# The expert loop's buffers move off the gate buffer, the first blocks' last gates are read on chip, and ScalarE's queue carries the last write-out

## The reference, cut to what matters

```python
def peer(h, w_query, sub_keys, expert_u, expert_v):        # 16384 experts of one neuron each
    q = (hf @ w_query).reshape(T, N_PEER_HEADS, 2, PEER_KEY_DIM // 2)
    s = jnp.einsum('thpk,hpnk->thpn', q, sub_keys)
    s1, i1 = lax.top_k(s[:, :, 0], PEER_TOPK)
    s2, i2 = lax.top_k(s[:, :, 1], PEER_TOPK)
    ...
    top_s, pos = lax.top_k(cand, PEER_TOPK)
    g = jax.nn.softmax(top_s.astype(jnp.float32), axis=-1).astype(h.dtype)
    ...
        a = jax.nn.gelu(jnp.einsum('tkd,td->tk', expert_u[ix], hx), approximate=False)
        return jnp.einsum('tk,tkd->td', gx * a, expert_v[ix])
```

## Time and profile before

| what | value |
|---|---|
| median of 3 runs | 1886.51 us (1883.4 to 1887.89) |
| the profiled execution | 1885.99 us, its span 1884.2 us |
| busy: PE, PEld, DVE, ACT, POOL | 92%, 79%, 78%, 36%, 51% |
| mean granted TensorE clock | 0.971 |
| DMA over the span | 520.92 MB, mean 276 GB/s |
| gate phase ends, loop's first scores, first sums | 751.4, 758.6, 791.0 us |
| last matmul of the loop | about 1848 us |

### The profile page before, as it was taken

The page is one execution under the profiler, slowest core; times in us unless marked ns, Lnnn a source line. Parts: engine busy times, 40 slices in busy tenths (PEclk is TensorE's granted clock), DMA queues, the critical chain, the costliest instruction groups (busy, mean ns, idle before and its releaser), DMA issues.

```text
span 1884.2 us, 29934 instructions
## 1 busy us (share of the span) xinstructions
PE 1739.1 (92%) x9942; PEld 1486.7 (79%) x9942; DVE 1474.6 (78%) x2936; ACT 683.9 (36%) x1145; POOL 961.2 (51%) x838
## 2 busy tenths in 40 slices
PE   5999988699799998499999999999999999999994
PEld 2767656377788886399999999999898998999993
DVE  0732057247968665799999999999999998999997
ACT  1222146110166768133333333333333333333331
POOL 1111000000067687288777777777566665666661
PEclk8999999899999999699999999999999999999997
DMA  9455110500006555999999999999999999999993
GB/s 356 154 198 218 46 57 1 212 23 13 23 1 133 116 111 118 297 392 406 406 407 395 407 407 407 407 407 407 388 403 399 403 402 390 389 405 407 406 406 136
DMA packets 253576, 520.92 MB, mean 276 GB/s; under 512 B 113987, under 2 KB 131011, under 8 KB 252229
## 3 DMA queue, kind: packets, MB, share of 16 engines
q1 hardware_dynamic: 178048, 249.00, 37.3%
q0 software_dynamic: 73728, 268.47, 36.0%
q10 hardware_dynamic: 1734, 2.60, 0.4%
HBM read 488.55 MB, written 31.46 MB: 276 GB/s over the span
## 4 chain that ended last, share of the span: by engine, by line
PE 52%; DVE 20%; issue 12%; DMA 8%; ACT 3%; SPq 2%; DVEq 1%; POOL 1%; POOLq 0%; PEldq 0%; ACTq 0%
PE ps L1758 9%; PE ps L1757 9%; PE ps L1756 9%; DVE arena L1331 9%; PE ps L1632 6%; DMA U_in<-in_expert_uT 4%; DVE V_lo L1273 4%; PE ps L1683 4%; PE ps L1613 3%; DMA arena_w<-in_w_mod 2%; PE ps L1461 2%; PE ps L1462 2%; PE ps L1465 2%; PE ps L1509 1%; DMA arena_w<-in_w_in 1%
## 5 line engine op out<-in xcount | busy, mean ns | idle before, releaser
L1756 PE MATMUL ps<-hT_hi,U_hi 128*128 128x384 f32 x1024 | 344.3, 336 | 7.8 <-DVE arena L1124 7.8
L1758 PE MATMUL ps<-hT_hi,U_lo 128*128 128x384 f32 x1024 | 344.3, 336 | 0.0
L1757 PE MATMUL ps<-hT_lo,U_hi 128*128 128x384 f32 x1024 | 343.7, 336 | 0.0
L1756 PE MATMUL ps<-V_hi,C_hi 128*128 128x512 f32 x768 | 301.7, 393 | 29.3 <-DVE C_lo L1308 29.3
L1758 PE MATMUL ps<-V_hi,C_lo 128*128 128x512 f32 x768 | 303.6, 395 | 0.0
L1757 PE MATMUL ps<-V_lo,C_hi 128*128 128x512 f32 x768 | 303.1, 395 | 0.0
L506 POOL DMA_INDIRECT arena<-in_expert_u,idxn x128 | 176.4, 1378 | 74.3 <-issue 38.2
L506 POOL DMA_INDIRECT arena<-in_expert_v,idxn x128 | 160.6, 1254 | 104.0 <-DVE arena L1331 55.4
L1756 PEld LDWEIGHTS ps<-hT_hi,U_hi 128*128 128x128 f32 x1024 | 192.8, 188 | 12.9 <-issue 8.0
L856 ACT ACTIVATE act_t<-ps 128x384 f32<-128x384 f32 x128 | 63.0, 492 | 368.9 <-PE ps L1758 368.8
L1757 PEld LDWEIGHTS ps<-hT_lo,U_hi 128*128 128x128 f32 x1024 | 192.8, 188 | 4.9
(11 more groups left out here) (240 smaller groups left out, 3237.6 us busy)
## 6 DMA issues: line engine op xcount, KB each, us to landing
U_in<-in_expert_uT SPq DMA_DIRECT2D x128, 512.0 KB, 9.5
V_in<-in_expert_v SPq DMA_DIRECT2D x128, 512.0 KB, 6.6
arena_w<-in_w_mod SPq DMA_DIRECT2D x12, 2048.0 KB, 12.0
gate_in<-gates_scratch SPq DMA_DIRECT2D x128, 192.0 KB, 7.8
gates_scratch<-arena_w SPq DMA_DIRECT2D x5, 4096.0 KB, 21.4
arena_w<-in_w_in SPq DMA_DIRECT2D x4, 2048.0 KB, 8.8
arena_w<-in_w_query SPq DMA_DIRECT2D x1, 7168.0 KB, 21.0
arena_w<-in_w_out SPq DMA_DIRECT2D x2, 2048.0 KB, 10.4
```

The costliest lines, as they stand in the source:

```text
L1756: nc.tensor.matmul(out, hi, rhi, start=start, stop=False)
L1757: nc.tensor.matmul(out, hi, rlo, start=False, stop=False)
L1758: return nc.tensor.matmul(out, lo, rhi, start=False, stop=stop)
```

## The change

- `V_in`, `V_hi`, `gate_in` and `act_t` go to the place of `h2T` and two of the `lhs1` buffers, `V_lo` to the place of the ranking's scratch, `C_hi` and `C_lo` to the place of `lhs1` and `rhs1`. In `gbuf`'s place lie now `rows_late`, `H2s`, `fing` and `XF`. `gbuf`'s first four columns stay free (`first_gates`).
- The last half write-out is one DMA, issued by ScalarE after the last eviction.
- For n = 0 to 3 the gates come in two DMAs: 320 tokens from HBM (`spilled_gates`) and the last 64 straight from `gbuf` (`fresh_gates`). SyncE's first turns are written out by hand; the loop begins at 3. `H2s` is loaded before it.
- SyncE's `break` still stands behind the wait for the last eviction.
- GpSimd's seventh row waits for the whole write-out, as before.
- VectorE ranks all four groups among the last block's gate rows, then come hT_lo and both U_lo with a quad between them, then `select` with two quads. ScalarE makes both `U_hi` at quad 20 and the last exponential at quad 28.
- VectorE waits for the last product and gates ahead of `split_v(0, 0)`.

```diff
...
@@ -181,6 +180,23 @@
...
         w_hi = [w_hi_first] + [w_hi_next] * (IN_CH - 1)
+        with ExitStack() as loop:
+            def loop_at(name, lo, shape):
+                loop_end[0] = lo + math.prod(shape[1:])
+                return loop.enter_context(nc.sbuf_tensor(name, shape, f32r))
+            def loop_gap(name, hi):
+                loop.enter_context(nc.sbuf_tensor(name, [P, hi - loop_end[0]], f32))
+            loop_end = [0]
+            loop_gap("to_V_lo", XO + 3 * D)
+            V_lo = loop_at("V_lo", XO + 3 * D, [P, 2, D])
+            loop_gap("to_V_hi", MO + 2 * D)
+            V_hi = loop_at("V_hi", MO + 2 * D, [P, 2, D])
+            loop_gap("to_C_hi", WO + NKEY * P)
+            C_hi = loop_at("C_hi", WO + NKEY * P, [P, 2, TD])
+            loop_gap("to_C_lo", CO + 14336)
+            C_lo = loop_at("C_lo", CO + 14336, [P, 2, TD])
         arena = sb("arena", [P, WO])
...
@@ -240,16 +255,18 @@
...
         accS = cutout(XO, 2 * D).rearrange("p (s d) -> p s d", s=2)
-        H2s = cutout(XO + 2 * D, D)
+        def pairs_at(lo, n):
+            return cutout(lo, 2 * n).rearrange("p (j n) -> p j n", j=2)
+        V_in, gate_in, act_t = pairs_at(MO, D), pairs_at(MO + 4 * D, TD), pairs_at(MO + 5120, TD)
+        first_gates = sb("first_gates", [P, 4 * P])
+        rows_late = sb("rows_late", [P, 2, D])
+        H2s = sb("H2s", [P, D])[:, :]
+        fing = sb("fing", [P, D])[:, :]
+        XF = sb("XF", [P, NBLK, D])
+        gap = sb("gap", [P, CO - WO - 4 * P - 9 * D])
         h2row = (H2[0], H2s)
-        XF = cutout(MO, 5120).rearrange("p (b d) -> p b d", b=NBLK)
-        V_in, gate_in = sb("V_in", [P, 2, D]), sb("gate_in", [P, 2, TD])
-        act_t = sb("act_t", [P, 2, TD])
-        C_hi, C_lo = sb("C_hi", [P, 2, TD], f32r), sb("C_lo", [P, 2, TD], f32r)
-        V_hi, V_lo = sb("V_hi", [P, 2, D], f32r), sb("V_lo", [P, 2, D], f32r)
-        rows_late = sb("rows_late", [P, 2, D])
-        gap = sb("gap", [P, CO - WO - 4096 - 2048 - 8 * TD - 2 * D])
...
@@ -393,40 +409,53 @@
...
             for b in range(1, NDEN + 1):
-                if b == NDEN:
-                    sp.wait_ge(s_fill2, B2.total)
-                    for j in range(2):
-                        load_u(j, j)
                 for half in range(2):
...
                     if b == NDEN and half:
-                        for e in range(3):
-                            part = slice(PIECES[e], PIECES[e + 1])
-                            sp.dma_start(gates_d[part, :, TD - P // 2:TD].rearrange("i p t -> p i t"),
-                                         gbuf[:, part, P // 2:P]).then_inc(s_glast[e], 16)
                         break
...
                                  gbuf[:, :, t0:t0 + P // 2]).then_inc(s_gout[half], 16)
+                if b + 1 == NDEN:
+                    sp.wait_ge(s_fill2, B2.total)
+                    for j in range(2):
+                        load_u(j, j)
+            def spilled_gates(n, j):
+                sp.dma_start(gate_in[:, j, 0:TD - P // 2], gates_d[n, :, 0:TD - P // 2]).then_inc(s_gin[j], 16)
+            def fresh_gates(n, j):
+                sp.dma_start(gate_in[:, j, TD - P // 2:TD], gbuf[:, n, P // 2:P]).then_inc(s_gin[j], 16)
+            sp.wait_ge(s_hTlo, 1)
+            for j in range(2):
+                load_v(j, j)
+            sp.wait_ge(s_gout[0], 16 * NDEN)
+            sp.wait_ge(s_gout[1], 16 * (NDEN - 1))
+            for j in range(2):
+                spilled_gates(j, j)
             for n in range(2, 4):
...
                 load_u(n, n % 2)
-            sp.wait_ge(s_gout[0], 16 * NDEN)
-            sp.wait_ge(s_gout[1], 16 * (NDEN - 1))
-            sp.wait_ge(s_glast[0], 16)
+            sp.wait_ge(s_gev, QUADS * NDEN)
             for j in range(2):
-                load_v(j, j)
-                load_gates(j, j)
-            for e in (1, 2):
-                sp.wait_ge(s_glast[e], 16)
+                fresh_gates(j, j)
             for n in range(2, 4):
...
                 load_v(n, n % 2)
-            sp.wait_ge(s_c, 1)
-            load_gates(2, 0)
-            sp.wait_ge(s_gate, NBLK)
+            for n in range(2, 4):
+                sp.wait_ge(s_c, n - 1)
+                spilled_gates(n, n % 2)
+                fresh_gates(n, n % 2)
+                sp.wait_ge(s_ulo, n + 1)
+                load_u(n + 2, n % 2)
+                sp.wait_ge(s_vlo, n + 1)
+                load_v(n + 2, n % 2)
+            sp.wait_ge(s_gout[1], 16 * NDEN)
+            sp.wait_ge(s_c, 3)
+            load_gates(4, 0)
             sp.wait_ge(s_h2out, 16)
+            sp.dma_start(H2s, h2_d).then_inc(s_h2in, 16)
...
@@ -439,9 +468,8 @@
...
             turns = PAIRS // 8
-            with sp.Fori(2, turns) as i:
+            with sp.Fori(3, turns) as i:
                 streams(i)
-            sp.dma_start(H2s, h2_d).then_inc(s_h2in, 16)
             for b in range(NBLK):
...
@@ -514,8 +542,8 @@
...
-                            pool.wait_ge(s_gout[0], 16 * NDEN)
-                            pool.wait_ge(s_glast[2], 16)
+                            for half in range(2):
+                                pool.wait_ge(s_gout[half], 16 * NDEN)
                             pool.sem_inc(s_staged, 1)
...
@@ -813,6 +841,11 @@
...
             softmax_exp(1)
+            def split_u(n, r, k):
+                act.wait_ge(s_uin[r], 16 * k)
+                act.copy(U_hi[:, r], U_in[:, r]).then_inc(s_uhi, 1)
             for n in range(2, NBLK):
...
@@ -824,7 +857,10 @@
...
                                  h2T[:, 1:1 + NDEN].rearrange("p b k t -> p k b t")).then_inc(s_hThi, 1)
-                    if p == QUADS - 4 and bd != NDEN:
+                    if p == HALFQ + 4 and n + 1 == NBLK:
+                        for j in range(2):
+                            split_u(j, j, 1)
+                    if p == QUADS - 4:
                         softmax_exp(n)
...
@@ -834,11 +870,6 @@
...
-            def split_u(n, r, k):
-                act.wait_ge(s_uin[r], 16 * k)
-                act.copy(U_hi[:, r], U_in[:, r]).then_inc(s_uhi, 1)
...
@@ -865,10 +896,9 @@
...
-            split_u(0, 0, 1)
-            split_u(1, 1, 1)
-            softmax_exp(NBLK - 1)
-            act.wait_ge(s_glast[1], 16)
+            act.wait_ge(s_gev, QUADS * NDEN)
+            act.dma_start(gates_d[:, :, TD - P // 2:TD].rearrange("i p t -> p i t"),
+                          gbuf[:, :, P // 2:P]).then_inc(s_gout[1], 16)
             split_v(0, 0, 1, True)
...
@@ -1214,13 +1244,12 @@
...
-            def ranking(n, b, bd, keys_share, pairs_share, select_share):
+            def ranking(n, b, bd, keys_share, pairs_share):
                 for g in range(4):
...
                 dve.wait_ge(s_step, steps[0])
-                select(n, bd, select_share)
...
@@ -1274,30 +1303,26 @@
...
                 bd = dense_at(n)
-                if bd != NDEN:
-                    ranking(n, n, bd, (1, 1, 0), (0, 1, 0), (1, 1, 1, 2))
-                else:
-                    for g in range(3):
-                        key_tops(n, g, bd, (1, 2, 1) if g else (0, 1, 1))
-                        dve.wait_ge(s_step, steps[0])
-                        pair_tops(g, bd, ((1, 1, 1), (0, 1, 0), (1, 1, 0))[g])
+                ranking(n, n, bd, (1, 1, 0), (0, 1, 0))
+                if bd == NDEN:
+                    gate_quads(bd, 1)
                     dve.wait_ge(s_hThi, 1)
...
                                       ALU.subtract).then_inc(s_hTlo, 1)
+                    gate_quads(bd, 1)
                     split_u(0, 0)
-                    ranked(n, 3)
+                    gate_quads(bd, 1)
                     split_u(1, 1)
-                    dve.wait_ge(s_step, steps[0])
-                    select(n, 0)
+                select(n, bd, (1, 1, 0, 0) if bd == NDEN else (1, 1, 1, 2))
                 gate_weights(n)
...
                     n = i * 2 + j
-                    dve.wait_ge(s_gin[j], 16 * (i + 1))
+                    dve.wait_ge(s_gin[j], 32 if isinstance(i, int) and i == 0 else 16 * (i + 3))
                     dve.wait_ge(s_ge, n + 1)
...
@@ -1365,9 +1390,9 @@
...
+            dve.wait_ge(s_gq, QUADS * NDEN)
+            dve.wait_ge(s_gate, NBLK)
             split_v(0, 0)
-            dve.wait_ge(s_gate, NBLK)
-            dve.wait_ge(s_gq, QUADS * NDEN)
             experts(0, False, dot_row(0))
...
```

More of the change, by code:

```diff
@@ L34 @@
 NB1 = NKEY
-PIECES = (0, 40, 72, NKEY)
 NDEN = 3
@@ L211, in program @@
         squared = rhs_more.rearrange("p t n -> p (t n)")
-        fing = cutout(MO + 5120, 1024)
         wq7 = cutout(BO + 1024, 2048)
@@ L316, in program @@
         s_gq = sem("s_gq"); s_gev = sem("s_gev"); s_gout = [sem(f"s_gout{i}") for i in range(2)]
-        s_glast = [sem(f"s_glast{i}") for i in range(3)]
         s_hThi = sem("s_hThi"); s_hTlo = sem("s_hTlo"); s_acc0 = sem("s_acc0")
```

## The result

The changed kernel takes 1893.78 us (median of 6 runs, 1892.66 to 1896.18), the kernel before 1883.78 us beside it (median of 6, 1883.19 to 1887.89): ratio 1.0049, 95% interval 1.0036 to 1.0062. It is slower by half a per cent. The profiled execution of after took 1894.71 us with a span of 1892.9 us, 8.7 us more than that of before. The forecast was 1896.4 us, slower, range 1883 to 1903.

The account below looks back on a forecast made before the run. TensorE, busy throughout from about 800 us, makes the loop a train of fixed length, so its last standstill sets the end. Block 2 +7.8, clock +2.6, rest 0: +10.4 on 1885.99 gives 1896.4 us, range 1883 to 1903.

Parts of the forecast that it names:

- The gate phase: Last gate block: VectorE's added two-input work slows GpSimd's back-to-back gate quads, moving the last eviction from 751.4 to 762.
- E: End of the gate phase's last eviction, 751.4 in the kernel before; forecast between 755 and 765, taken as 762.
- Rival 1: Last gate block: VectorE, not GpSimd, sets the gates' end, at 755; time 1889.4; chance 0.14.
- Three quarters, or the whole: Gate rows: VectorE's two-input work costs GpSimd 0.75 of its length; losing all would end the gates some 3 us later.
- First sums: Loop start, block 0: fresh gates at E + 16.5, sums at E + 21 = 783, against 790.96, a gain of 8.
- The seventh row: GpSimd's gather behind the write-out, which lands last at E + 42; row there at E + 48.7, gather at 803 to 805.
- block 2: Start of its sums in the loop: E + 56 = 818.0 against 810.17, so +7.8 us.
- Rival 2: Write-out keeps a share beside the loads and lands at E + 35; block 2 at 811, time 1889.4; chance 0.11.
- rival 3: Write-out lands by E + 29, first sums set the start: 1878; 1882.4 combining Rival 1 and Rival 2; chance 0.13 together.
- Clock: TensorE's restart at granted clock 0.50, hidden at the first sums and paid again at block 2: +2.6 us.
- The second standstill: TensorE, after the first sums, stands 16 us ahead of the sums of block 2, with the clock at 0.50.
- The rest: New buffer places and addresses, earlier H2s loads, one wait fewer: zero, between -0.5 and +3 us.

Follow-up runs that it names:

- e1: The kernel before with only the new order of the last gate block; buffers, loads and write-outs as before: 1895.47 us, ratio 1.0064.
- e5: The changed kernel with VectorE's last five gate quads ahead of hT_lo, both U_lo and the selection, ScalarE's last exponential behind the gates: 1888.64 us, ratio 1.002.
- e13: The kernel before with 126 idle products on TensorE between the scores of block 1 and the first sums: 1884.23 us, ratio 0.9986.
- e10: The kernel before with 100 idle products on TensorE behind the scores of block 1: 1884.25 us, ratio 0.9991.
- e8: e5 with SyncE's break ahead of the wait for the last eviction, so V0 to U3 load earlier: 1881.54 us, ratio 0.9986.
- e11: e2 with SyncE's break ahead of the wait for the last eviction, as in e8: 1875.76 us, ratio 0.9958.
- e14: e11 with 75 idle products on TensorE between the scores of block 1 and the first sums: 1878.27 us, ratio 0.9969.
- e9: e8 with SyncE waiting for the write-out's landing ahead of V3: 1880.46 us, ratio 0.9976.
- e12: e11 with SyncE waiting for the write-out's landing ahead of V3, as in e9: 1877.17 us, ratio 0.9959.
- e4: The changed kernel with SyncE waiting for the write-out's landing ahead of V2 and the loads after it: 1892.01 us, ratio 1.005.
- e2: The changed kernel with the old order of VectorE and ScalarE in the last gate block: 1881.73 us, ratio 0.9985.
- e3: The changed kernel with gathered rows 7 and 8 of the first pass placed so that no gather waits for the write-out: 1897.91 us, ratio 1.0079.

## Why the prediction was right, step by step

**The gate phase, right in mechanism; the tenth is luck.** E was forecast at 762 and is 762.03. The forecast counted 39.1 us from a last score at 722.89. The score came 1.0 us earlier, and from there to E it was 40.2 us. So the term was 1.1 us too small (11.7 us measured, 10.6 forecast), and a profiled execution that was ahead before the last gate block hid it. It was GpSimd, as argued: its last four quads were forecast at 24.5 us in sum (13.0 own work and 11.5 lost beside VectorE) and took 25.1. Rival 1 (VectorE sets E, 755) is refuted by these rows: VectorE's last quad ended at 750.4, and E waited for GpSimd's. e1 shows that this term alone costs all of the loss. e5 turns it round: with VectorE's quads pulled forward, 6.2 us of the 11.7 go.

**Three quarters, or the whole.** The cleanest row is that of before: 2.6 us lost beside the 3.51 of hT_lo, 0.74. In e5 the last quad takes 8.21 us, against 3.17 for the one ahead of it, 5.0 lost. In its time lie 2.9 us of hT_lo (which began 0.45 us earlier), 2.35 of two U_lo and some 1.6 of short two-input steps of the selection: the loss is 0.95 of the long ones, or 0.73 of all. The Trainium skill ("SBUF — State Buffer", section "SBUF: two separate sides") has GpSimd locked out for the whole length of such an operation. The rows of before show most of it, not all; those of e5 don't decide, since they don't tell what the short steps cost.

**First sums, near.** Forecast 783, measured 784.59, from fresh gates at E + 18 (forecast E + 16.5).

**The seventh row, mechanism right, two sizes off.** Gather forecast at 803 to 805, issued at 802.02, since the write-out landed at E + 39.2 and not E + 42. The other traffic was priced right: 8.65 MB moved beside it, 21.2 us at 408 GB/s, forecast 21.5. The write-out's own 19.0 us and the 1.3 us of margins were too long: the earlier trace rows shows it at 221 GB/s from 771 to 774, but alone from 780 to 786 in after it moved 290 GB/s, and from 765 to 768 in before 282 to 299 as well. From its landing to VectorE's take the row took 5.2 us and not 6.7. Together 4.2 us too late in the sum. Against that, rows eight and one came late behind it (0.57 and 0.74 us of waiting; forecast 0.3): 8.3 us from the seventh row to the sums, not 7.3. So block 2 came at +4.6 and not +7.8. Rival 2 had the right direction (E + 35) but not the size, and rival 3 (E + 29 or less) did not come about. In no kernel whose write-out went by ScalarE's queue did it land before E + 29.

**Clock, right in kind.** Forecast 2.6, measured 2.05 in after (10.36 less 8.31), 2.5 by e13 in before. The second standstill (11.61 us, forecast 16) had its own restart at the low clock, as forecast.

**The rest, mis-sized.** Forecast 0, range up to +3. The profiled executions differ by 8.7 us: 6.7 at block 3, 2.7 gathered up to 1650 us (all but 0.2 of it between 1300 and 1650), and 0.7 given back at the end. The 2.7 us were in no term. The change isn't shown to cause them: the idle time between 1300 and 1650 us is 4.3 to 6.4 us in the four profiled kernels with the old buffers and loads (before, e1, e10, e13) and 3.6 to 7.9 us in the ten with the new ones, so what differs between before and after lies inside the scatter of kernels whose loop is the same.

The two errors of +3.2 and -2.7 nearly cancel; with block 2 at its measured place and 0.5 less of clock the sum would have been 1892.7 (1896.4 - 3.2 - 0.5), and the median is 1893.78. The base was off as well: 1885.99 was one profiled execution, and the median of before beside the changed kernel is 1883.78. The forecast was +10.4 us; the two profiled executions differ by 8.7 and the two medians by 10.0. So 2.2 of the 2.6 us between 1896.4 and 1893.78 are the base, and the closeness of the sum is in part luck. The forecast's direction did not hang on it.

What the prediction didn't see is the way out. It named the break behind the last eviction's wait as a fact, and took the seventh row as the next wait, but it didn't ask what V0 to U3 would give if they left before E. e8 and e11 show 5 to 7 us. By the ratios, e11 is 0.9% below the changed kernel.

## What to carry to other kernels

When a wait is removed, look for the transfer behind it and ask who asks for it next: here each relief (the buffers, the ring, the order) moved the stall to another reader of the same write-out or to what was held back for it, and what moved the time was less traffic in front of it, or an earlier end of its producer. An order that hides in one block of a phase behind an engine's slack is dear in the last block, where that engine runs piece behind piece: here 11.7 us. Count a clock penalty for each standstill, but look at what sets the stretch behind it before you count on winning it back: in e14 most of it was gone by block 5.

## What the runs showed of the hardware

**A write-out of short runs yields to nearly everything.** Its 4.19 MB in 256-byte runs moved at 290 GB/s alone at first (after, 780 to 786) and at 221 later (before, 771 to 774). In after, from its issue to 780 us, its queue moved 0.39 MB (22 GB/s) while the gathers moved 3.15 and SyncE's loads 2.97. From issue to landing it took 29.1 us in e9, 29.6 in e12, 29.8 in e14, 30.0 in e11, 33.6 in e4, 34.3 in e8, 34.7 in e2, 39.2 in after, 40.4 in e5 and 62.8 in e3, by how much else was let in front of it: at the worst a mean of 67 GB/s. The Trainium skill ("DMA: Bandwidth & Descriptors", section "Queues, rings and completion order") describes a turn by packets among the queues. The trace agrees that it has a share while the others load, and shows it to be small. The forecast, which let it land behind the sum of all transfers, was 2.8 us late in after.

**A gather's issue is dearer beside VectorE.** GpSimd's indirect DMAs take 0.94 us to issue where VectorE stands still (after, 802.02) and 1.79 and 1.98 us in e2, where it was busy with two-input work. With eight rows to refill this can be one part of the late rows behind the seventh; no run tests it.
